# VectorE's copy of turned products between two maxima, and five other reorderings

## The reference, cut to what matters

```python
p = softmax(concat([q @ k_latent, q @ k_context]) * scale)   # per head
x = x + g1 * (concat([a_lat, b_lat, c_lat, d_lat]) @ w_out[l])
h2 = modulate(rms_norm(x, norm_ffn[l]), sh2, sc2)
x = x + g2 * moe_ffn(h2, ...)        # shared expert + sum of gated experts
```

## Time and profile before

| | us |
|---|---|
| median of the runs | 1605.51 |
| the profiled execution's own time | 1604.38 |
| its span | 1602.5 |
| TensorE busy | 1553.2 (97%) |
| VectorE busy | 837.6 (52%) |
| ScalarE busy | 427.2 (27%) |
| GpSimd busy | 195.6 (12%) |

### The profile page before, as it was taken

One profiled execution on the slowest core, in us unless ns is written; L12 is line 12 of the kernel. 1 busy time (PEld: TensorE's weight loads), 2 busy tenths in 40 slices (PEclk: granted clock), 3 DMA queues, 4 the chain that ended last, 5 costly groups with the idle time before them and its releaser, 6 DMA issues.

```text
span 1602.5 us, 26470 instructions
## 1 busy us (share of the span) xinstructions
PE 1553.2 (97%) x10102; PEld 1052.1 (66%) x10102; DVE 837.6 (52%) x1796; ACT 427.2 (27%) x922; POOL 195.6 (12%) x348
## 2 busy tenths in 40 slices
PE   6999999999999999999999999999999999999996
PEld 4655446766665577788888655556666667788883
DVE  1323424567676677454545722524667656644346
ACT  1322113455554410100000412114555541000001
POOL 0111102000000000212121110211000000121212
PEclk9999999999999999999999999999999999999998
DMA  9561132721001387689897861144701034588884
GB/s 353 193 248 53 53 54 64 251 104 40 15 27 40 118 319 274 217 325 347 322 340 284 295 227 54 53 65 153 254 1 41 22 118 166 205 295 306 320 323 189
DMA packets 113617, 285.61 MB, mean 178 GB/s; under 512 B 33008, under 2 KB 42926, under 8 KB 103726
## 3 DMA queue, kind: packets, MB, share of 16 engines
q1 hardware_dynamic: 102134, 263.13, 47.5%
q0 software_dynamic: 10800, 20.99, 3.4%
q10 hardware_dynamic: 584, 0.14, 0.0%
HBM read 265.47 MB, written 40.37 MB: 191 GB/s over the span
## 4 chain that ended last, share of the span: by engine, by line
PE 91%; DVE 3%; issue 2%; SPq 1%; DMA 1%; ACT 1%; POOL 0%; DVEq 0%; POOLq 0%; ACTq 0%
PE S L1277 18%; PE S L1658 16%; PE B L1434 9%; PE S L1360 8%; PE S L1669 8%; PE PT L1380 6%; PE B L1411 6%; PE B L1298 3%; PE B L1181 2%; PE PT L1583 2%; PE S L1298 2%; PE S L1522 1%; PE S L1542 1%; DMA arena<-in_w_in 1%; PE B L1515 1%
## 5 line engine op out<-in xcount | busy, mean ns | idle before, releaser
L1277 PE MATMUL S<-arena 128*128 128x512 f32 (+3 forms) x768 | 297.7, 538 | 3.0 <-DMA arena<-in_w_in 2.3
L1658 PEld LDWEIGHTS S<-arena 128*128 128x128 f32 x2304 | 265.3, 193 | 16.7 <-issue 16.7
L1658 PE MATMUL S<-arena 128*128 128x128 f32 x2304 | 265.7, 276 | 0.0
L1277 PEld LDWEIGHTS S<-arena 128*128 128x128 f32 x768 | 140.6, 191 | 124.1 <-issue 103.6
L1047 ACT ACTIVATE arena<-S,nmax 128x768 f32<-128x768 f32 (+1 forms) x200 | 161.8, 812 | 148.7 <-DVE nmax L2150 118.6
L2150 DVE TENSOR_REDUCE nmax<-S 128x1 f32<-128x768 f32 (+1 forms) x168 | 133.1, 825 | 69.2 <-PE S L1360 60.2
L1434 PE MATMUL B<-arena 128*128 128x512 f32 x320 | 150.7, 598 | 0.0
L1360 PE MATMUL S<-arena 64*128 64x512 f32 (+5 forms) x624 | 142.0, 494 | 5.0 <-ACT arena L1047 5.0
L1380 PEld LDWEIGHTS PT<-cst,arena 128*128 128x128 f32 x832 | 93.8, 140 | 58.4 <-issue 55.8
L1669 PE MATMUL S<-arena 128*128 128x512 f32 x288 | 129.5, 592 | 0.0
L1380 PE MATMUL PT<-cst,arena 128*128 128x128 f32 x832 | 121.8, 278 | 3.0 <-issue 2.7
(11 more groups left out here) (323 smaller groups left out, 1765.5 us busy)
## 6 DMA issues: line engine op xcount, KB each, us to landing
arena<-in_w_mod SPq DMA_DIRECT2D x24, 2048.0 KB, 10.4
arena<-in_moe_w_gate SPq DMA_DIRECT2D x36, 1024.0 KB, 7.4
arena<-in_moe_w_up SPq DMA_DIRECT2D x36, 1024.0 KB, 8.9
arena<-in_moe_w_down SPq DMA_DIRECT2D x36, 1024.0 KB, 5.6
arena<-in_w_in SPq DMA_DIRECT2D x6, 2048.0 KB, 8.0
arena<-y SPq DMA_DIRECT2D x20, 512.0 KB, 5.8
arena<-mod SPq DMA_DIRECT2D x16, 512.0 KB, 7.2
arena<-in_tokens SPq DMA_DIRECT2D x12, 512.0 KB, 9.9
```

Of the source, the lines that this page charges most:

```text
L1277: mm = pe.matmul(ubank[u % 4][:, c0:PANEL_W[p]], hT[:, k, t * P:(t + 1) * P], panel[p][:, k, c0:], start=k == 0, stop=k == KT - 1)
L1658: mm = pe.matmul(to, wgu[b][:, w, k * DE + h * P:k * DE + (h + 1) * P], XT[b][:, k, :], start=k == 0, stop=k == KT - 1)
```

## The change

Six edits: a piece of the projection moves from step 2 to step 1, and one from step 6 to step 7. VectorE's copy of a first product stands between the two maxima in steps 2 and 6. In the last steps some pieces stand ahead of the values, with their number split anew. ScalarE squares ahead of the exponentials in step 1, and VectorE scales in step 1 instead of 2. In layer 1 GpSimd scales the shared down weights in two halves, behind its last reciprocal root. In layer 1 the weight table stands ahead of the first gathered turning, with two idle products before that turning and two behind it.

```diff
--- before.py
+++ after.py
@@ -104,8 +104,10 @@
 
 JOBS = {3: ("g", 0), 4: ("c", 0), 5: ("n", 0), 7: ("m", 0), 8: ("c", 1), 9: ("n", 1), 10: ("g", 1), 11: ("m", 1)}
 CARRIERS = [("d", 3), ("m", 1)]
-PIECES = {0: (0, 2), 2: (2, 5), 3: (5, 6), 4: (6, 8), 6: (8, 11), 7: (11, 12), 8: (12, 14), 9: (14, 16)}
-LAST_PIECES = {0: (0, 4), 1: (4, 5)}
+PIECES = {0: (0, 2), 1: (2, 3), 2: (3, 5), 3: (5, 6), 4: (6, 8), 6: (8, 10), 7: (10, 12), 8: (12, 14), 9: (14, 16)}
+COPY_BETWEEN = (2, 6)
+LAST_PIECES_FIRST = {0: (0, 1), 1: (3, 5)}
+LAST_PIECES = {0: (1, 3)}
 JOB_NO = {job: i for i, job in enumerate(JOBS.values())}
 V_JOB_NO = {job: i for i, job in enumerate(job for job in JOBS.values() if job[0] != "c")}
 NJ = len(JOBS)
@@ -1080,6 +1082,8 @@
                 nt = tiles_of(l)
                 for n in range(NS * nt + 3):
                     t, k = divmod(n, NS)
+                    if t >= 2 and k == 1:
+                        x1_square(t - 2)
                     if t < nt:
                         exps(t, k)
                     for nb in nb_units_in(l, n):
@@ -1089,8 +1093,6 @@
                         out_diff(job[0], job[1][1])
                     if 1 <= n <= NS * nt:
                         out_product(*divmod(n - 1, NS))
-                    if t >= 2 and k == 1:
-                        x1_square(t - 2)
                 gend = T * l + nt
 
                 def gate_exp(gi, b):
@@ -1199,10 +1201,10 @@
                         tr = pe.transpose(PT[:, j * P:(j + 1) * P], xs[:, j, :], ident)
                     tr.then_inc(s["hT_tr"], 1)
 
-                def idle_products(n=8):
+                def idle_products(n=8, bank=S1):
 
                     for _ in range(n):
-                        pe.matmul(S1[0:32, 0:32 * KT], cs[:, 0, :], cs.rearrange("p k x -> p (k x)"), start=True, stop=True)
+                        pe.matmul(bank[0:32, 0:32 * KT], cs[:, 0, :], cs.rearrange("p k x -> p (k x)"), start=True, stop=True)
 
                 if l == 0:
                     for n in range(4):
@@ -1459,6 +1461,9 @@
                     if two and n < NS:
                         product(tp, kp, 0)
                     job = job_at(l, n)
+                    if t == nt and k in LAST_PIECES_FIRST:
+                        for piece in range(*LAST_PIECES_FIRST[k]):
+                            out_piece(t - 1, piece)
                     if job:
                         values(*job)
                     if two and n >= NS:
@@ -1472,7 +1477,7 @@
                         mod_product(l, FAR_STEPS[n], B7)
                     if after:
                         product(tp, kp, 1)
-                for piece in range(LAST_PIECES[1][1], KT):
+                for piece in range(LAST_PIECES_FIRST[1][1], KT):
                     out_piece(nt - 1, piece)
 
                 gend = T * l + nt
@@ -1671,8 +1676,6 @@
                     mm.then_inc(s["e_d"], 1)
 
                 def e_block(blk, u, b, more, first):
-                    if l and first and b == 0:
-                        weight_table()
                     pe.wait_ge(s[f"e_g_in{b}"], 16 * (u + 1 + NBK[0] // 2 * l))
                     if first and b == 0:
 
@@ -1695,8 +1698,11 @@
                     e_in(blk, b, 1)
 
                 if l:
+                    weight_table()
                     pe.wait_ge(s["s_ob"], gend - 2)
+                    idle_products(2, B7)
                     e_turn(0, 0, 0, False)
+                    idle_products(2, B7)
                 for b in range(2):
                     e_block(b, 0, b, True, True)
                 with pe.Fori(1, pairs_1) as i:
@@ -1824,6 +1830,13 @@
                     diff_rstd(t, 1)
                 x1_rstd(nt - 2)
                 x1_rstd(nt - 1)
+                if l:
+
+                    pool.wait_ge(s["s_w_in"], 16 * 4 * (l + 1))
+                    pool.wait_ge(s["s_g2_in"], 16 * 3 * (l + 1))
+                    for k in range(2):
+                        ins = pool.tensor_tensor(swd_g2[0][:, k, :], swd[:, k, :], g2[:, 0, :], ALU.mult)
+                    ins.then_inc(s["s_scaled"], 1)
                 nt = T if l == 0 else TL
                 gend = T * l + nt
 
@@ -2130,6 +2143,8 @@
                             att_ch.done(dve.tensor_reduce(dtmp[:, 2 * m:2 * m + 1], (S0, S1)[m][:, SEQ:nk], AX.X, ALU.max))
                     for m in range(2):
                         Sm = (S0, S1)[m]
+                        if m and k in COPY_BETWEEN:
+                            out_product(t, k - 1)
                         dve.wait_ge(s["scored"], scores_done(l, t, k) + int(context_first) + m + 1)
                         if m == 0 and k in (5, 9):
 
@@ -2234,7 +2249,7 @@
                         gated(t - 1, 0)
                     if t < nt:
                         maxima(t, k)
-                    if 1 <= n <= NS * nt and STEPS[(n - 1) % NS][0] != "d":
+                    if 1 <= n <= NS * nt and STEPS[(n - 1) % NS][0] != "d" and not (t < nt and k in COPY_BETWEEN):
                         out_product(*divmod(n - 1, NS))
                     job = job_at(l, n)
                     if job and job[1][0] != "c":
@@ -2251,7 +2266,7 @@
                             mod_gain(l, 1)
                     if t >= 2 and k == 0:
                         x1_sum(t - 2)
-                    if t >= 2 and k == 2:
+                    if t >= 2 and k == 1:
                         h2_scale(t - 2)
                     if t >= 2 and k == 3:
                         h2_shift(t - 2)
@@ -2459,8 +2474,6 @@
                 h2_shift(nt - 1)
                 dve.wait_ge(s["s_w_in"], 16 * 4 * (l + 1))
                 dve.wait_ge(s["s_g2_in"], 16 * 3 * (l + 1))
-                if l:
-                    s_scale_down(0)
                 for t in range(2, nt):
                     s_half(t)
                     s_gate_mul(t - 2)
```

## The result

The kernel after took 1607.30 us (median of 20 runs, 1604.02 to 1612.10), the kernel before 1604.56 (20 runs, 1602.37 to 1607.42) beside it: ratio 1.0018, 95% interval 1.0011 to 1.0026. The change makes the kernel 2.7 us slower; the forecast was 0.8 faster. The kernel after also spreads more: its 20 executions lie within 8.1 us and five of them took 1610.6 to 1612.1, where the 20 of the kernel before lie within 5.1. One execution of a later experiment (the one with VectorE scaling early) was in a slow state, 2305.42 us at a granted clock of 0.655, and is left out of its ratio. The profiled execution took 1607.56, span 1605.7, against 1604.38 and 1602.5.

A forecast was written before the change was run, and what follows sets the result against it. TensorE, busy almost throughout, was taken as the bound, through its queue, waits and clock. Attention +6.2, last pieces -2.9, GpSimd's scaling 0 and gather -4.1 gave -0.8, so 1604.7 us, range 1599 to 1610.6.

The forecast's parts named there:

- Attention, +6.2: Latent tiles, both layers: moved pieces, copy between maxima and earlier residual scaling together add 3.1 us per layer, +6.2.
- copy hidden: Rival: VectorE's copy between the maxima costs nothing, attention priced at 0, total -7.0, 1598.5 us; chance 0.22.
- What the scaling gives, the later exponential takes: Step 3 of attention: moving residual scaling saves VectorE time, but step 2's exponential is later; a wait of 0.6 stays.
- GpSimd scales the weights, taken as 0: Layer 1, shared expert's last turning: VectorE's product starts first, the turning starts at 1346.5 as today; 0, bound -1.4.
- GpSimd goes first: Rival, layer 1 shared expert: GpSimd's product precedes VectorE's, last turning 2.4 late, another clock fall; +5.0, 1610.5 us; chance 0.22.
- Clock behind that wait, +3.4 in the rival: After a 3.8 us TensorE wait at the shared expert's last turning, layer 1, the granted clock falls: +3.4; rival's chance 0.22.
- Last pieces, -2.9: Last attention steps: pieces ahead of late values fill TensorE's waits, -2.1 in layer 1 and -0.8 in layer 0.
- Gather, -4.1: Layer 1 gathered rows: table and idle products save 0.7 of waiting and 3.4 by keeping the clock at 2.4 GHz.
- The sum: Whole kernel: +6.2 - 2.9 + 0 - 4.1 = -0.8 us, applied to the median 1605.51.
- that term at its best, -1.4: Lower bound for GpSimd's weight scaling in layer 1: TensorE's wait of 1.40 at the shared expert's last turning goes.

The follow-up runs named there:

- the one with VectorE scaling early: Kernel after without the copy between maxima, with old pieces, VectorE scaling the shared weights before its last gate product, no GpSimd products: 1601.19 us, ratio 0.9978.
- late scaling: Kernel after plus one line: GpSimd waits for VectorE's last shift of layer 1 before scaling the shared weights; 1604.05 us, ratio 0.9995.
- the table alone: Kernel before with only the weight table moved ahead of the turning of gathered rows, without idle products; 1601.92 us, ratio 0.9982.

## Why the prediction was wrong

**Attention, +6.2: right.** The pair of profiles has 3.03 + 2.91 = 5.9; the copy taken out of the finished change gives 6.4. The rival "copy hidden" fell. What the sum hid is that it is the difference of a good edit and a bad one: the earlier scaling gives 2.6 by itself, the copy costs 8.3 by itself. "What the scaling gives, the later exponential takes" came out, but should have led to the two edits being priced apart.

**GpSimd scales the weights, taken as 0: the step that failed.** The prediction let VectorE's product start first and gave no row for that order; it only noted, under the rival, that VectorE's start is within 0.04 of the release. The trace after has GpSimd 0.02 ahead; the mutual exclusion was right and the order wrong. The price is 2.08 in the trace (TensorE's wait is 3.48 instead of 1.40). Against late scaling it is 3.25 by the medians, of which 1.40 could have been gained on before. The rival "GpSimd goes first" had a chance of 0.22. It named the mechanism and 2.4 for it; without its fall of the clock it makes +1.6 on before, where +2.7 was measured. Its 1607.1 is near the 1607.30 only because it was added to a median of 1605.51, and the 20 executions beside the kernel after gave 1604.56. The Trainium skill, "SBUF — State Buffer", section "Who interferes with whom", has the two kinds of instruction exclude each other for their whole length, and all three traces agree: 3.41 and 3.25 with GpSimd first, 1.28 and 3.25 with VectorE first, 1.28 and 1.22 apart.

**Clock behind that wait, +3.4 in the rival: not in the profile.** 1.00 behind a wait of 3.48. It may come in some executions, among them the five over 1610 us; no profile shows one. The mean clock over all executions is 0.9946 for after, 0.9954 with the scaling back on VectorE and 0.9959 with late scaling. As an estimate, 0.0013 of some 1605 us is 2.1 us, so a good part of the 3.25 may be clock and not wait, and the medians cannot part the two. This stays open.

**Last pieces, -2.9: right in the trace of that edit alone (-2.0 and -0.7), not by the time.** The median fell by 0.45 and the interval ends at 1.6. The three waits were sized rightly; what gave their gain back in most executions stays open. In the profiled one it was the wait of 1.64 and 1.7 more of the clock's fall.

**Gather, -4.1: right.** -3.77 in the pair of profiles, -4.0 by the medians of the run with that edit alone.

**The sum.** -0.8 becomes +3.2 in the pair of profiles by 2.08 at the turning, 1.47 at the start of the program, 0.3 at the gather and 0.2 between the layers. The 1.47 belongs to the two executions. By the medians 3.5 are missing (-0.8 to +2.7). GpSimd's products account for 1.5 to 1.8 of them (the run with the scaling back on VectorE), and the last pieces for 2.4 more (0.45 for 2.9), each uncertain by a microsecond and more. With late scaling the time is 1.0 under the kernel before beside it, where the forecast with that term at its best, -1.4, would give -2.2. So the term taken as 0 is shown to be wrong and its repair takes the loss away, but it is not the whole of the 3.5.

## What to carry to other kernels

When work is moved to another engine, ask who starts first and what each waits for: if the two are released within a fraction of a microsecond and exclude each other, order them with a semaphore, the critical one first; here that was one line and 3.3 us by the medians, 3.7 in the profiles. Idle time of an engine is a place for work only from the moment that the work's inputs have landed. Price edits that share a step one by one before taking their sum: here one of three in attention was worth 2.6, one cost 8.3, and one had no purpose without the other.

## What the runs showed of the hardware

- Where GpSimd's 128x1024 products run, a VectorE product that reads two SBUF tiles waits for one of them to end, and they then alternate: 3.41 and 3.25 in place of 1.28 and 1.22. A VectorE addition that reads one SBUF tile (L2286, 128x256) waits too, 2.07 in place of 0.28, while the reciprocal behind it takes its usual 1.75 beside GpSimd's second product, and the copy ahead of it, out of the bank of turned products, its usual 0.68. Meanwhile GpSimd's pair takes 5.63, or 6.45 when VectorE is first, or 4.73 when VectorE mostly computes something else.
- A single idle stretch of TensorE does not tell whether its clock falls: none after 3.48, one after 2.77 that followed a wait of 1.75, one after 2.59 and one around stretches of 0.88 and 0.98 (the table alone). At the gather all six profiles without idle products have a fall, which loses 3.4 us or more by the windows of 5 us, and none of the eight with them has one. Idle products are not the only way: by its median the table alone already gives 3.3 of the 4.0.
- Three places differ between the profiles where their code is equal: the clock's fall near 34 us (the scores of the table's first row stand between 252.2 and 255.5 in the fourteen profiles), the shared expert of layer 0 (16.9 to 19.3 us from the first tile's turning to the third's), and a wait ahead of a modulation product near 1130 (0 to 1.64). A single pair of profiles can't carry a difference of 3 us unless it is cut into stretches.
